# The first MLP product as seven quarter products in blocks 1 to 7, with weight sums made by adding DMAs

## The reference, cut to what matters

```python
D_MODEL = 1024; SEQ = 512; D_FF = 4 * D_MODEL
hm = rms_norm(x, mlp_norm_g[l])                       # [512, 1024]
x = x + jnp.square(jax.nn.relu(hm @ w_mlp_in[l])) @ w_mlp_out[l]   # [1024, 4096], then [4096, 1024]
return rms_norm(x, final_norm_g)
```

## Time and profile before

| | us |
|---|---|
| three executions, median (lowest to highest) | 737.99 (737.86 to 738.38) |
| the profiled execution, own time | 737.4 |
| its span, first to last instruction | 735.7 |
| MLP, from the first hidden matmul to the last matmul | 399.4 to 728.6 |

### The profile page before, as it was taken

How to read it: one execution, slowest core, us unless ns; L and a number is a source line. 1 busy time by engine, 2 the same in 40 slices (tenths; PEclk the granted TensorE clock), 3 DMA queues, 4 the chain that set the end, 5 groups by cost and what they waited for, 6 DMA issues and landing times.

```text
span 735.7 us, 9813 instructions
## 1 busy us (share of the span) xinstructions
PE 718.9 (98%) x3490; PEld 603.1 (82%) x3490; DVE 513.0 (70%) x791; ACT 378.4 (51%) x595; POOL 109.2 (15%) x145
## 2 busy tenths in 40 slices
PE   5999999999999999999999999999999999999996
PEld 4788878888888888888888888888888888888885
DVE  5686996777896754337435695868778695968964
ACT  6463545867854665543224654545364544545432
POOL 4421241012212456400200100000000000000002
PEclk9999999999999999999999999999999999999999
DMA  8555123644997653112713242241515051332002
GB/s 298 153 99 150 58 90 83 132 117 105 224 221 176 144 119 110 58 58 86 257 58 129 101 142 87 88 141 57 171 36 190 2 171 57 116 113 86 30 1 114
DMA packets 25051, 85.12 MB, mean 116 GB/s; under 512 B 2712, under 2 KB 4920, under 8 KB 25016
## 3 DMA queue, kind: packets, MB, share of 16 engines
q1 hardware_dynamic: 19104, 67.87, 27.5%
q0 software_dynamic: 3312, 12.06, 8.8%
q10 hardware_dynamic: 2600, 4.72, 2.9%
HBM read 68.91 MB, written 3.67 MB: 99 GB/s over the span
## 4 chain that ended last, share of the span: by engine, by line
PE 95%; ACT 2%; DVE 1%; DMA 1%; issue 0%; POOL 0%; SPq 0%; POOLq 0%; DVEq 0%; ACTq 0%
PE bank L1520 20%; PE bank L1522 20%; PE bank L1521 20%; PE bank L1566 9%; PE bank L1570 8%; PE bank L1567 8%; PE bank L1751 2%; PE bank L1528 2%; PE bank L1659 2%; DMA xs<-x 1%; PE bank L1733 1%; PE bank L1732 1%; PE bank L1649 1%; PE bank L1650 1%; PE bank L1710 0%; PE bank L1671 0%
## 5 line engine op out<-in xcount | busy, mean ns | idle before, releaser
L1520 PE MATMUL bank<-hTh,whi 128*128 128x512 f32 (+1 forms) x264 | 102.8, 389 | 0.5 <-DVE hTl L1045 0.5
L1522 PE MATMUL bank<-hTh,wlo 128*128 128x512 f32 (+1 forms) x264 | 102.7, 389 | 0.0
L1521 PE MATMUL bank<-hTl,whi 128*128 128x512 f32 (+1 forms) x264 | 102.7, 389 | 0.0
L683 ACT CAST whi<-raw 128x1024 fp32r<-128x1024 f32 x58 | 60.3, 1041 | 41.3 <-PE bank L1522 40.7
L1566 PE MATMUL bank<-hTh,whi 128*128 128x512 f32 x192 | 78.0, 406 | 1.0 <-DVE hTl L1045 1.0
L1520 PE MATMUL bank<-whi,ah 128*128 128x512 f32 x196 | 76.2, 389 | 0.0
L1521 PE MATMUL bank<-wlo,ah 128*128 128x512 f32 x196 | 76.2, 389 | 0.0
L1522 PE MATMUL bank<-whi,al 128*128 128x512 f32 x196 | 76.2, 389 | 0.0
L1570 PE MATMUL bank<-hTl,whi 128*128 128x512 f32 x192 | 75.1, 391 | 0.0
L1567 PE MATMUL bank<-hTh,wlo 128*128 128x512 f32 x192 | 74.9, 390 | 0.0
L934 ACT ACTIVATE rt<-bank 128x512 f32<-128x512 f32 x32 | 19.1, 598 | 85.8 <-PE bank L1522 85.8
(11 more groups left out here) (245 smaller groups left out, 1625.6 us busy)
## 6 DMA issues: line engine op xcount, KB each, us to landing
raw<-slabs SPq DMA_DIRECT2D x87, 512.0 KB, 3.5
br<-slabs SPq DMA_DIRECT2D x32, 512.0 KB, 3.5
wlo<-raw POOLq DMA_DIRECT2D x23, 512.0 KB, 4.9
xs<-x SPq DMA_DIRECT2D x4, 512.0 KB, 5.2
y<-x ACTq DMA_DIRECT2D x1, 2048.0 KB, 8.8
bias_rows<-rbias ACTq DMA_DIRECT2D x1, 1536.0 KB
out<-ys SPq DMA_DIRECT2D x3, 512.0 KB, 2.6
bt<-bias_rows ACTq DMA_DIRECT2D x1, 1024.0 KB, 6.1
```

The lines of the kernel that those rows point to most:

```text
L683: act.copy(whi[s][:, :], raw[s][:, :]).then_inc(hi_done, 1)
L1520: pe.matmul(dst, lh, rh, start=start, stop=False)
L1521: pe.matmul(dst, lh, rl, start=False, stop=False)
L1522: return pe.matmul(dst, ll, rh, start=False, stop=stop)
```

## The change

The first block keeps the plain first product (`hidden`). In blocks 1 to 7 the first product is made of seven quarter products as well (`up_product`): W_in of a block in four quarters (512 input features x 256 hidden features), h in four quarters (512 features x 256 tokens). Each is 4 k x 2 halves x 3 matmuls of 256 columns, 24, so 168 a block. Sums of products are formed in PSUM: products 0, 2, 4 and 6 follow each other on bank 3 (2, 4 and 6 add to what is there), 1 and 3 on bank 2, and 5 has bank 0. Between two of them ACT copies the partial sum to SBUF (`keep`), and DVE adds such a copy to a bank to form a quadrant of the hidden block (`quadrant`); ACT then takes relu and square of it.

The sums of h are made once, in the first block: POOL adds hTh and hTl (8 adds of 128x512, tile hf32), DVE forms four sums of 128x1024 (`t_sum`), and ACT and DVE split them (`t_round`, `t_rest`). The sums of weights, of W_in and now of W_out too, are made by six adding DMAs of POOL a block, each 512 KB from SBUF to SBUF (`sums`), and one DVE sum (`w_sum`) in place of four. W_in comes in 7 loads of a quarter a block in place of 4 of a slab (r11, r12, r21, r22 into the raw slots, and a second copy of three into s1, s2, s4), each in rows of 2 KB; W_out in 4 as before. A slab to split comes up 14 times a block (`WPB`) in place of 11. The tiles ah and al of a quarter of hv are three in place of seven. The first block writes the accumulators by copies (POOL's five memsets fall away), and the seven products of W_out are another form of the same scheme, in another order, with another recombination in `last_` (ten additions of a half row block to y from accumulators in place of eight).

```diff
-        def in_use(m, it):
-
-            return it * USE_B[m] + MB
+        NST = NFB - 2
+        WPB = 14
+        W0 = 4 + 7
...
+        UP_BANK = (3, 2, 3, 2, 3, 0, 3)
+        PBANKS = ((4, 5), (0, 1), (2, 3), (0, 1), (2, 3), (0, 1), (6, 7))
+        KEPT = (0, 6)
...
+        u_src = [r11, s1, s2, s4, r21, r12, r22]
+        a_src = [two(sa), a_part(0, 0), two(sb), a_part(0, 1), two(sx), two(sa), a_part(1, 1)]
+        w_src = [br["12"], br["11"], d1, br["21"], br["11"], br["22"], br["21"]]
...
+        h_hi = [hTh3[:, 0:4, 0:256], t_hi[0], t_hi[1], hTh3[:, 4:8, 256:512], t_hi[2], hTh3[:, 4:8, 0:256], t_hi[3]]
...
+            for k in MLP_K:
+                b, u = mlp_bank[k]
+                pool.wait_ge(free[b], u + 1)
+                pool.tensor_tensor(hf5[:, k // 4, :, k % 4, :], hTh3[:, k, :].bitcast(F32).rearrange("p (s t) -> p s t", s=2),
+                                   hTl3[:, k, :].bitcast(F32).rearrange("p (s t) -> p s t", s=2),
+                                   ALU.add).then_inc(S["tf_done"], 1)
...
+            def sums(it):
+
+                pool.wait_ge(S["wt_done"], it + 2)
+                pool.wait_ge(br_in["11"], it * 16 + 32)
+                add_into(br["12"], br["11"], ds_in[3])
+                pool.wait_ge(raw_in[ring(0)], raw_count(0, it + 1))
+                pool.wait_ge(raw_in[ring(2)], raw_count(2, it + 1))
+                add_into(r21, r11, us_in[3])
+                pool.wait_ge(sl_in[1], it * 16 + 32)
+                pool.wait_ge(raw_in[ring(3)], raw_count(3, it + 1))
+                add_into(s1, r22, us_in[1])
+                pool.wait_ge(lo_done, NLO + out_op(1, it))
+                pool.wait_ge(ds_in[3], it * 16 + 32)
+                add_into(br["11"], d1, ds_in[2])
+                pool.wait_ge(sl_in[2], it * 16 + 32)
+                pool.wait_ge(us_in[1], it * 16 + 32)
+                add_into(s2, s1, us_in[2])
+                pool.wait_ge(lo_done, NLO + out_op(3, it))
+                pool.wait_ge(ds_in[2], it * 16 + 32)
+                add_into(br["21"], br["11"], ds_in[4])
+                pool.wait_ge(sl_in[4], it * 16 + 32)
+                pool.wait_ge(us_in[2], it * 16 + 32)
+                add_into(s4, s2, us_in[4])
...
+            def second_half(it):
+                ended(0, it)
+                hi_out(4, it)
+                a_hi(3, it, "hv_done", 4)
+                ended(1, it)
+                hi_out(5, it)
+                a_hi(4, it, "s_done", 3)
...
+            def up_part(it):
+                hi_up(3, it)
+                keep(0, rt[0], it)
+                hi_up(4, it)
+                act.wait_ge(S["al_done"], it * 7 + 3)
+                keep(1, sb, it)
+                hi_up(5, it)
+                keep(2, rt[1], it)
+                hi_up(6, it)
...
+                quadrant(3, rt[1], 0, 1, 1.0, it, 1)
+                up_full(4, it)
                 hi_out(0, it)
-                relu(1, it)
-
-                act.wait_ge(S["wt_done"], it * 4 + 2)
+                quadrant(4, sb, 1, 1, -1.0, it, 2)
+                a_hi(0, it, "s_done", 1)
+                up_full(5, it)
                 hi_out(1, it)
-                a_hi(0, it, "hv_done", 2)
-                relu(2, it)
-
-                act.wait_ge(S["wt_done"], it * 4 + 4)
+                quadrant(5, rt[0], 0, 0, 1.0, it, 3)
+                a_hi(1, it, "hv_done", 3)
+                quadrant(6, rt[1], 1, 0, -1.0, it, 0)
                 hi_out(2, it)
-                a_hi(1, it, "s_done", 1)
-                relu(3, it)
-
+                a_hi(2, it, "s_done", 2)
                 hi_out(3, it)
...
+            def second_half(it):
                 a_lo(3, it)
-                gather(0, it)
-                dve.wait_ge(S["al_done"], it * 7 + 2)
-                s_sum(sa, a_part(0, 1), two(sx), ALU.subtract, it, 0, 3)
+                lo_out(4, it)
+                gather(1, it)
+                lo_out(5, it)
                 a_lo(4, it)
-                lo_out(4, it)
                 gather(2, it)
-                lo_out(5, it)
+                lo_out(6, it)
                 a_lo(5, it)
                 gather(3, it)
                 a_lo(6, it)
-                lo_out(6, it)
                 gather(4, it)
-                lo_in(0, it + 1)
+                lo_up(0, it + 1)
                 gather(5, it)
-                lo_in(1, it + 1)
...
+            def first_():
+                lo_op(4, ring(3), raw[ring(3)])
+                w_sum(-1)
+                lo_out(0, -1)
+                dve.wait_ge(S["tf_done"], KD_)
+                t_sum(f11, f11, f12, ALU.subtract, 0)
+                t_sum(f12, f22, f12, ALU.subtract, 1)
+                t_sum(f22, f11, f22, ALU.add, 2)
+                t_sum(f21, f22, f21, ALU.subtract, 3)
+                a_lo(0, -1)
...
+            def block_(it):
+                lo_up(3, it)
+                lo_up(4, it)
+                w_sum(it)
+                lo_up(5, it)
+                lo_up(6, it)
+                quadrant(3, 2, rt[1], it)
+                quadrant(4, 1, sb, it)
+                lo_out(0, it)
+                s_sum(sa, a_part(1, 1), a_part(1, 0), ALU.subtract, it, 2)
+                a_lo(0, it)
+                quadrant(5, 0, rt[0], it)
+                lo_out(1, it)
+                s_sum(sb, a_part(0, 0), a_part(1, 0), ALU.subtract, it, 3)
+                a_lo(1, it)
+                s_sum(sx, two(sb), a_part(1, 1), ALU.add, it, 0, 2)
+                lo_out(2, it)
+                a_lo(2, it)
+                s_sum(sa, two(sx), a_part(0, 1), ALU.subtract, it, 4, 3)
+                lo_out(3, it)
+                second_half(it)
...
+            def up_product(q, it):
+                s, b = ring(q), UP_BANK[q]
+                wh, wl = slab_view(whi, s, 8), slab_view(wlo, s, 8)
+                pe.wait_ge(lo_done, NLO + up_op(q, it))
+                if q in T_OF:
+                    pe.wait_ge(S["tlo_done"], T_OF[q])
+                pe.wait_ge(free[b], up_use(q, it))
+                onto = q in (2, 3, 4, 6)
+                for m in range(2):
+                    dst = bank[b][:, m * 256:(m + 1) * 256]
+                    for k in range(4):
+                        pe.matmul(dst, wh[:, 4 * m + k, :], h_hi[q][:, k, :], start=m + k == 0 and not onto, stop=False,
+                                  skip_group_check=True)
+                        pe.matmul(dst, wl[:, 4 * m + k, :], h_hi[q][:, k, :], start=False, stop=False, skip_group_check=True)
+                        ins = pe.matmul(dst, wh[:, 4 * m + k, :], h_lo[q][:, k, :], start=False, stop=k == 3,
+                                        skip_group_check=True)
+                ins.then_inc(full[b], 1)
```

More of the change, by code:

```diff
@@ L1466, in last_ @@
-                mix(acc[6], acc[6], acc[1], ALU.add, 0)
-                mix(acc[3], acc[3], acc[5], ALU.add, 0)
+                    dve.wait_ge(*product_full(0, q, NST - 1))
+                    dve.tensor_tensor(d1[:, q * T:(q + 1) * T], bank[4 + q][:, :], acc[4][:, q * T:(q + 1) * T],
+                                      ALU.add).then_inc(free[4 + q], 1)
+                lo_up(5, it)
+                lo_up(6, it)
+                quadrant(3, 2, rt[1], it)
+                quadrant(4, 1, sb, it)
@@ L1848, in _ @@
+            for m in range(4):
+                hidden(m)
+            for pos in range(7):
+                out_product(pos, -1, True, False)
+            with pe.Fori(0, NST - 1, 1) as it:
                 block_(it)
```

583 lines of the change are left out of this document (360 added, 223 removed).

## The result

The changed kernel takes **772.11 us** (median of 4 runs, 769.18 to 774.77), the kernel before 737.92 (737.82 to 738.38) beside it: ratio 1.046, 95% interval 1.042 to 1.050. The profiled execution's own time is 771.08, its span 769.3. The direction was forecast, the size was not: 34 us more where 10.4 were predicted.

What follows compares the result with a forecast made beforehand. PE bounds the kernel (98% busy), but after the change the DVE and ACT chain with a late add makes it wait: 737.4 + 2.4 (first block) + 7.8 (loop) + 0.2 (end) = 747.8, plus 0.6 for the median: 748.4 us, range 732 to 758.

Steps and rivals of the forecast that it cites:

- A 256-column matmul takes 0.120 us: First product on PE: 168 such matmuls take 20.16 us in place of 21.76, a gain of 1.6 us a block.
- Rival 4: First product on PE: half the columns take half the time, 0.113 us a matmul, giving 743.4 us; chance 0.03.
- the page's 109 ns: First product on PE: the Trainium skill's 262 cycles for a 256-column matmul; by it 740.6 us.
- The chain of ACT and DVE: Loop block: handovers to the CAST of d1 at 23.6 us, then DVE without a gap to 35.4; block ends at 40.9.
- The add of d1 onto br11: Loop block: issued at 20.7, takes 4.5 + 1.5 = 6.0 us, lands at 26.7, shifting DVE's run 1.2 us; block 42.1.
- three pieces of waiting: Loop block: PE idle some 3 us in all, ahead of products 3, 4 and 5, released by DVE's gathers.
- the whole 1.6 us is given back: Loop block: PE's 1.6 us gain is lost because rests of W_out slabs wait for a ring slot until up-products 4 to 6.
- The first block: First MLP block: PE work unchanged, products 1 and 3 start late behind ACT and DVE work; +2.4 us.
- The end: Last block and end: PE 1.6 us less, but DVE's additions to y put the last y at 44.0 against 42.2; +0.2 us.
- The add is never late: Loop blocks: the add onto br11 lands in time, blocks of 40.9, 741.2 us in all; chance 0.15.
- PE stays the bound: Loop blocks: PE never waits for DVE, ACT or the add; 726.8 us, or 731 with first block and end; chance 0.18.
- The DMA engines decide: Loop blocks: DMA engines 82% busy, adds land after 8.0 us, shift 3.2 in place of 1.2, 760 us; chance 0.09.

Runs made afterwards that it cites:

- e9: e4 plus further order edits and e8's; on ScalarE and VectorE gathers and tokens-side operations put ahead of weight CASTs and rests awaiting transfers; 734.15 us, ratio 0.9947.
- e2: The changed kernel without the transfer adding d1 onto br11 and its waits, plain br11 used instead, so part of the output differs; 749.40 us.
- e1: The changed kernel with twelve 512-column matmuls on an all-zero stationary tile put behind the third W_out product of every block; 766.49 us.
- e12: The changed kernel with POOL's transfers in the order br12, r21, br11 (+= d1), s1, br21, s2, s4; 763.33 us.
- e8: The changed kernel with only POOL's chain for the row norms of y moved behind the first block's seven transfers; 771.22 us.
- e4: The changed kernel with the fifth and sixth W_out products of every block exchanged, banks and gathers with them; 758.60 us.
- e10: e9 with VectorE's six additions of kept sums to the right half of y moved behind the four adding banks to the left half; 733.39 us, ratio 0.9938.
- e11: e10 with POOL's transfers in the order of e12; 737.04 us (10 runs).

## Why the prediction was wrong

The profiled span grew by 33.6 us: 5.5 up to the start of the second block (2.4 predicted), 26.2 in the six loop blocks (7.8), and 1.9 from the last block's start to the end of the span (0.2).

- **A 256-column matmul takes 0.120 us: right.** The changed kernel's rows have 535.12, 535.23, 535.35 and 535.47 as starts, and e9's blocks, all PE time, take 39.5 us: 168 x 0.12 + 84 x 0.2267 = 39.2, and 0.3 more. The gain is 1.3 a block, not 1.6; what the 0.3 is, no run shows. Rival 4, and the page's 109 ns with it, is refuted.
- **The chain of ACT and DVE: right to 0.5 us.** It was to hand over the CAST of d1 at 23.6 us of the block and end the block at 40.9. The CAST ended at 23.6 (557.80 is 22.7 in) and without the add the block took 41.4.
- **The add of d1 onto br11: the mechanism right, its size off.** Issued at 20.7, 6.0 us long, landed at 26.7 was the step, from landings by the semaphore; by that measure it is 21.05, 6.5 to 8.1 (7.1 in the block shown) and 28.1. DVE's rounding rest waited 2.0 to 3.5 us where a shift of 1.2 was priced, and product 3 starts 32.4 us into the block in the mean, 2.7 later than without the add (29.7 in e2): 1.5 too little. The transfer to look at was not SP's load, which was put in as the 1.5 us of sharing, but the adding one 2 us ahead in the same queue, whose own issue hangs on a quarter load. That it comes at 18 to 20 us was not worked out.
- **A stall was priced at its own length only.** This is the step that failed in kind. The prediction summed three pieces of waiting to 3 us, ahead of products 3, 4 and 5; in fact they are one, of 3.5 to 5.0 us, since product 3's gather stands behind everything late. And each is followed by 3.4 us (once 6.8) at the 1.2 GHz level, a term that the sum doesn't have: 1.1 to 1.2 us a stretch in e1 and e12, 7 to 8 us over the six blocks. The Trainium skill (TensorE: Matmul & The Clock Gate, HAM oscillation — how this bites in real kernels) prices such a stretch at half its length, 1.7 us here; e1 and e12 show less, as part of it is waited out anyway.
- Together: 0.5 + 1.5 + 1.1 = 3.1 a block, 18.6 us, for the 18.4 missed in the loop. The 1.1 is what the part from product 3 to the block's end took more than in e2 (12.8 against 11.7 us in the mean).
- **The first block** was off by 3 us, 0.4 of it ahead of its first matmul (399.78 against 399.42). POOL's additions of h were said to be "over before the DVE sums of them are wanted". So they were: they ended at 409.15, and the DVE sums began at 412.44. But the transfer onto br12 was queued behind them and behind POOL's norm chain (to 413.7), issued at 413.70 (2.4 us earlier in e8), and ACT waited 5.53 us. The fall of the clock cost nothing here: e4's first block had none and ended at the same time, 445.8. The prediction had asked who waits for POOL's additions, not who stands behind them.
- **The end** was off by 1.7 us, and not by its sum. PE's part fell by 1.6 us, as worked out. DVE's row of additions was foreseen too: the first final scaling starts at 757.81, 41.0 us into the block (40.9 predicted), the last y at 760.87, 44.1 (44.0 predicted). But the prediction stopped there. Behind the last scaling both kernels' last output has landed after 3.4 us, and the program then ends with a DRAIN of POOL. Before and after, in the view of the closing line:

```profile
L76 POOLq DRAIN  x1: 2884/2884/2884, 730.9 to 730.9; - x1
```

```profile
L75 POOLq DRAIN  x1: 6067/6067/6067, 763.0 to 763.0; - x1
```

It starts 0.9 us ahead of the last scaling in both. So the span ends 3.85 us behind the start of that scaling before and 5.35 after: 1.5 us in which nothing is computed. The 5.35 is there in every run with all the adding DMAs (72 in the program, against 23 before); e2, with 65, has 4.77. That the DRAIN grows with the DMAs that POOL has issued fits these three, but was not tried by itself. Of the 3.4 us more behind TensorE that e10's expectation starts from (10.9 against 7.5), 1.5 are this.
- **Rivals.** "The add is never late" falls short too: with no add at all e2 takes 749.40, not 741. "PE stays the bound" is not this kernel; e9 shows it for the same arithmetic in another order, at 734.15 against 731 worked out. "The DMA engines decide" is refuted as a cause: in e9 they are 0.91 to 0.95 busy and PE never waits.
- Where the prediction said that "the whole 1.6 us is given back, because rests ... wait for a ring slot", e9 shows the weaker point: the same slots and the same work, and nothing given back. It took the order within the queues as given, correctly for the time, but the limit it named was not one.

## What to carry to other kernels

When a transfer is late, don't ask only who needs its data: list what stands behind the waiting instruction on its engine and needs nothing from it, above all what frees a bank or rounds another operand. Put those first; here that was worth 29 us, landing the transfer some 1 us sooner 9. A stall of TensorE of about 3 us or more mostly cost 1.1 to 1.2 us on top of its length here, so two edits that each leave 3 us of it are worth less than one that brings it to 1; and an order of issues on a queue is to be judged by all its waits, since an exchange of two that looked harmless cost 33 us.

## What the runs showed that was not expected

- The clock fell to 0.50 behind all twelve long stalls (3.4 to 5.2 us) in the loop blocks of the changed kernel and of e8, but not behind every stall of that size elsewhere: it stayed at 1.00 behind 3.17 us in e12_pool_order, 3.61 in e2_no_add and 3.67 in e4_swap (start to start, PE at full load before them), and fell behind 3.24, 2.82 (both e12), 2.42 (e4) and 2.39 (e1). So blocks of one program with nearly the same stall come out different, and its executions may too. That may be why the kernels with the long stall vary by 2.8 to 5.6 us over four runs, and e9 and e10 by 1.0; it was not tried by itself.
- Two adding DMAs of 512 KB on POOL's queue, issued 1.4 to 2.9 us apart, land 3.9 to 4.6 us apart; the first 4.3 to 5.0 us after its issue, as one with nothing beside it on the queue does (4.2 to 4.5, onto s2 in e2_no_add). In flight together they cost nearly their sum. With the order of e12 the second of two issued 0.5 us apart took 7.5 to 8.1 us, the first 5.3 to 5.8, so these landed 2.7 to 2.8 us apart: the 4.4 us that e11's expectation takes for all is not general.
- With the DMA engines over 0.9 busy through the loop (e9), the transfer onto br21 still landed 4.5 us after its issue.
